# Attention: a running minimum of negated scores on VectorE in place of a pass over the blocks' maxima

## What is computed

```python
s = jnp.einsum('bqhd,bkhd->bhqk', qi, k, preferred_element_type=jnp.float32) * sc
s = s + (Fi[:, :, :, None] - Ft[:, :, None, :])
s = jnp.where(kpos[None, :] <= qpos[:, None], s, -jnp.inf)
pr = jax.nn.softmax(s, axis=-1)
return jnp.einsum('bhqk,bkhd->bqhd', pr.astype(v.dtype), v)
```

## Time and profile before

| | us |
|---|---|
| median of 3 runs | 1343.44 |
| lowest and highest | 1336.95, 1344.19 |
| profiled execution, whole time | 1337.98 |
| its span in the trace | 1336.3 |
| PE busy | 1273.1 (95%) |
| VectorE busy | 713.6 (53%) |
| ScalarE busy | 566.0 (42%) |
| GpSimd busy | 181.6 (14%) |
| mean granted clock of TensorE | 0.981 |

### The profile page before, as it was taken

One profiled execution on the slowest core, in us unless ns is written; L12 is line 12 of the kernel. 1 busy time (PEld: TensorE's weight loads), 2 busy tenths in 40 slices (PEclk: granted clock), 3 DMA queues, 4 the chain that ended last, 5 costly groups with the idle time before them and its releaser, 6 DMA issues. The chain is left out here.

```text
span 1336.3 us, 19347 instructions
## 1 busy us (share of the span) xinstructions
PE 1273.1 (95%) x7007; PEld 1033.3 (77%) x7007; DVE 713.6 (53%) x1965; ACT 566.0 (42%) x1158; POOL 181.6 (14%) x193
## 2 busy tenths in 40 slices
PE   6899999999999999999979999999999995899997
PEld 1669988888888888888857777777777774788885
DVE  0646531353465121100059889899898997244444
ACT  2536521221221212111148778787787886111111
POOL 1223310100100100110000041032013115000000
PEclk9899999999999999999969999999999999899999
DMA  9636454131122344331176859749677974666662
GB/s 364 240 114 198 146 159 139 51 97 64 34 97 66 123 148 130 125 123 64 50 200 80 124 111 152 112 100 171 85 123 126 103 186 117 205 197 195 199 192 63
DMA packets 163836, 179.51 MB, mean 134 GB/s; under 512 B 35361, under 2 KB 125013, under 8 KB 159974
## 3 DMA queue, kind: packets, MB, share of 16 engines
q1 hardware_dynamic: 158478, 160.42, 48.9%
q10 hardware_dynamic: 5264, 17.86, 4.2%
HBM read 111.55 MB, written 66.69 MB: 133 GB/s over the span
## 5 line engine op out<-in xcount | busy, mean ns | idle before, releaser
L597 PE MATMUL prj_acc<-prj_hhi,til_whi 128*128 128x512 f32 (+1 forms) x800 | 286.3, 358 | 0.0
L599 PE MATMUL prj_acc<-prj_hlo,til_whi 128*128 128x512 f32 (+1 forms) x800 | 284.3, 355 | 0.0
L598 PE MATMUL prj_acc<-prj_hhi,til_wlo 128*128 128x512 f32 (+1 forms) x800 | 284.2, 355 | 0.0
L1589 DVE TENSOR_TENSOR att_wlo<-att_tps,att_whi 128x512 fp32r<-128x512 f32 (+1 forms) x336 | 185.1, 584 | 25.4 <-ACT att_whi L1542 23.6
L1542 ACT ACTIVATE att_whi<-att_tps 128x512 fp32r<-128x512 f32 (+1 forms) x336 | 164.1, 516 | 43.7 <-PE att_ops L1494 21.8
L599 PEld LDWEIGHTS prj_acc<-prj_hlo,til_whi 128*128 128x128 f32 x800 | 150.8, 188 | 21.3
L597 PEld LDWEIGHTS prj_acc<-prj_hhi,til_whi 128*128 128x128 f32 x800 | 150.9, 189 | 20.9
L598 PEld LDWEIGHTS prj_acc<-prj_hhi,til_wlo 128*128 128x128 f32 x800 | 150.8, 188 | 20.7
L1579 DVE TENSOR_SCALAR_CACHE_REDUCE att_wx<-att_sps 128x512 f32<-128x512 f32 (+4 forms) x164 | 94.0, 595 | 103.7 <-PE att_sps L1466 98.8
L1463 PE MATMUL att_sps<-att_ka,att_qa 128*128 128x512 f32 (+4 forms) x328 | 135.4, 413 | 10.9 <-DMA att_kb<-scratch_fkd 10.5
L1494 PE MATMUL att_ops<-att_whi,att_vt 128*128 128x512 f32 (+1 forms) x336 | 138.1, 415 | 1.0 <-DVE att_wlo L1589 1.0
(11 more groups left out here) (189 smaller groups left out, 2073.0 us busy)
## 6 DMA issues: line engine op xcount, KB each, us to landing
til_wraw<-in_w_in SPq DMA_DIRECT2D x20, 512.0 KB, 4.2
scratch_v<-val_vs SPq DMA_DIRECT2D x17, 512.0 KB, 4.8
val_xt<-in_x_prompt ACTq DMA_DIRECT2D x16, 512.0 KB, 4.4
ini_al<-in_w_ada SPq DMA_DIRECT2D x8, 1024.0 KB, 16.3
zin_zh<-scratch_z SPq DMA_DIRECT2D x16, 512.0 KB, 4.4
zin_zl<-scratch_z SPq DMA_DIRECT2D x16, 512.0 KB, 5.7
zin_xr<-in_x_prompt SPq DMA_DIRECT2D x16, 512.0 KB, 5.5
out_y_prompt<-yo_o ACTq DMA_DIRECT2D x16, 512.0 KB, 2.8
```

The source lines that it names most:

```text
L597: pe.matmul(out, w[0][:, k, :], hhi[:, k, cs], start=(k == 0), stop=False)
L598: pe.matmul(out, w[1][:, k, :], hhi[:, k, cs], start=False, stop=False)
L599: mm = pe.matmul(out, w[0][:, k, :], hlo[:, k, cs], start=False, stop=(k == KT - 1))
L1589: dve.tensor_tensor(wlo[b][0:x.keys, x.skip:x.width], tps[x.i % T_RING][0:x.keys, x.skip:x.width], raw(whi[b][0:x.keys, x.skip:x.width]), ...
```

## The change

Scores are copied with the factor -1 in place of 1, and the instruction takes the minimum instead of the maximum. From a row's second block on it starts from the result of the block before it (`before`, a 128x1 operand in memory), and so it waits for that block (`s_free`). The last block of a row writes to `nm` directly. The TENSOR_REDUCE, its semaphore `row_ok` and the function `rows_done` are gone. ScalarE waits for the row's last block by `s_free`, and its exponential takes the negated scores with scale -1. In the planner, the 100 that a row's last block cost more than others is gone. All later lines move up by 5, so line 1589 is 1584 in the new file, 1542 is 1537 and 1536 is 1531.

```diff
         if kind == "den":
             return 300, 120
-        return (170 if kind == "score" and x.last else 70) + 103 * (x.width if kind == "add" else x.n) // 100, 120
+        return 70 + 103 * (x.width if kind == "add" else x.n) // 100, 120
...
                 if kind == "exp":
-                    act.wait_ge(row_ok, rows_done(st) - sum(b.last for b in st.blocks) + 1
-                                + [b.row for b in st.blocks if b.last].index(x.row))
+                    act.wait_ge(s_free, ROW_END[st.index, x.row] + 1)
...
-                    act.activation(w, w, ACT.Exp, bias=nm[0:x.m, e, x.row:x.row + 1],
+                    act.activation(w, w, ACT.Exp, scale=-1.0, bias=nm[0:x.m, e, x.row:x.row + 1],
...
+                    before = None
+                    if x.b >= 1:
+                        dve.wait_ge(s_free, x.i)
+                        before = top[0:x.m, e, x.row, x.b - 1:x.b]
+                    here = nm[0:x.m, e, x.row:x.row + 1] if x.last else top[0:x.m, e, x.row, x.b:x.b + 1]
                     dve.tensor_scalar(weights(st, x.row, x.w0, x.n), sps[x.i % S_RING][0:x.m, 0:x.n],
-                                      1.0, None, ALU.mult, ALU.max,
-                                      accum_out=top[0:x.m, e, x.row, x.b:x.b + 1]).then_inc(s_free, 1)
-                    if x.last:
-                        dve.wait_ge(s_free, x.i + 1)
-                        dve.tensor_reduce(nm[0:x.m, e, x.row:x.row + 1], top[0:x.m, e, x.row, 0:x.b + 1], AX, ALU.max,
-                                          negate=True).then_inc(row_ok, 1)
+                                      -1.0, before, ALU.mult, ALU.min, accum_out=here).then_inc(s_free, 1)
```

## The result

| | before | after |
|---|---|---|
| median, us (8 runs each) | 1343.24 | 1349.20 |
| lowest and highest, us | 1336.95, 1345.35 | 1346.15, 1351.75 |
| ratio after to before | | 1.0047, 95% interval 1.0027 to 1.0066 |
| profiled execution: span, us | 1336.3 | 1349.9 |

The changed kernel is 6 us slower; 1345 had been forecast. The profiled execution of before lies low in its spread and that of after high, so their spans differ by more than the medians. The clock is the same (0.98) and the merge takes as long as it did; the time is in the attention.

The account below looks back on a forecast made before the run. VectorE's queue and its holes were taken to bound the attention: 5.1 us less work, 8.1 us more holes, its end 3.0 us later within slack. The merge, 1.5 us later, gave 1345 us from a 1343.44 median; range 1333 to 1355.

Parts of the forecast that it names:

- Scalars: VectorE, 172 blocks behind another of their row: reading one scalar from memory adds 0.06 us each, 10.3 us.
- The wait: VectorE, 77 blocks directly behind their row's previous block: each starts 0.115 us later, 8.9 us in all.
- work term: VectorE's work in the attention: 24.3 us of reduces off, 10.3 and 8.9 us added; 5.1 us less.
- The six holes: Ends of steps 5, 8, 11, 14, 17, 20: VectorE idles 2.49 us instead of 1.14, net +8.1 us.
- PE's lost time: PE starves about a microsecond in each hole and may not make it up: 0 to 2.4 us, taken as 0.
- The handover: Attention to merge: a SyncE, GpSimd, DMA chain starts the merge, 2.6 - 1.1 = 1.5 us later.
- The hook: Where the merge's chain hangs on VectorE in head 5: 5 x 1.35 - 4.1 = 2.6 us later.
- Step 20's early reciprocals: They come right behind the step's last block, ending SyncE's 6.7 us wait; DMA lets 1.1 us be won.
- the first (waits free): New waits and scalars cost VectorE nothing, work falls 14 to 24 us; 1333 us, chance 0.12.
- the second: The hole on VectorE is smaller or regained while the 1.14 us stalls go; about 1336 us, chance 0.14.
- the fourth: The DMA chain has more slack against VectorE, so the merge starts as before; 1343 us, 0.52 together with the forecast.
- The third: PE's lost microsecond is not regained and some 14 step starts lose 0.5 us each; 1352 us, chance 0.22.

Follow-up runs that it names:

- the case of the pairs: The blocks of two rows alternate, so none directly follows the one whose minimum it takes, planner costs adjusted; against the kernel before: 1327.81 us, ratio 0.9905.

## Why the prediction was right or wrong

- **What bounds:** right that VectorE's queue sets most of the pace. Reduces taken off and waits put on moved the time by 0.5 to 0.8 of their size, scalars by 0.3.
- **Reduces removed:** 0.19 us each as work, right; the sum took them at full worth, the chip gave half (12.3 of 25.8 us over the whole kernel).
- **Scalars:** 0.06 us each, right (742 for 680 ns); at the end they cost 3.2 of 11.5 us.
- **The wait: a term that was mis-sized.** The working took 0.115 us from the reduce's start in the earlier trace rows; the direct pairs take 0.20 to 0.21. In 77 pairs that is 0.09 x 77 = 7 us more, and turns the work term of -5.1 us into about +2. In the old order, over the whole kernel, it is 20.5 + 11.5 - 25.8 = +6.2 us, and +6.3 was measured. That this fits so well is luck: in the medians the three terms showed as 16.1 + 3.2 - 12.3 = +7.0, each at another share of its size.
- **The six holes:** place and mechanism right, 2.12 us for 2.49 forecast, and the 1.14 us waits did go. VectorE stands ahead of the reciprocals, for the exponentials, and not ahead of the subtraction for whi. All waits for ScalarE rose to 42.8 us (some 38 forecast). Missed: the six waits of 0.99 us at the ends of first steps (the same cause, reciprocals right behind a last block) and the knock-on. The attention's end was to move by 3.0 us in all; the order alone moved it by 14.8, both by 24 to 26.
- **PE's lost time taken as 0:** wrong for the attention. "It may not make it up" was the right half of that sentence: PE's waits for VectorE's subtractions ahead of its transposes rose from 9.6 to 16.5 us, and VectorE in turn waited for PE's second score product 5.5 us (1.1 before). What it is worth by itself no run shows.
- **The handover: a step that failed.** It is right for the kernel before, and for the new instructions in the old order, that the merge is set by a chain with a hook on VectorE further back and not by the attention's end. For the changed kernel it is wrong. The end of the attention was to move by 3.0 us "inside the 13.5 us of slack"; it moved by 24 to 26, used the slack up, and holds the merge in both profiles: by the addition at 1137.53 in one, by the last subtraction and value products in the other. The merge was to start 1.5 us later and started 10 to 15 us later in these two profiles. The other chain was late too: by the estimate above it would have held the merge 1 to 2 us short of that.
- **The hook** was to come 2.6 us later and came 10.4 (392.1 for 381.7). The old order with the new instructions has 10.5, so the instructions suffice for it: the work term, which stood in the hook with -4.1. With 0.205 us for each of the old order's 89 pairs, the prediction's counts give 10.3 + 18.2 - 24.3 = +4.2 there; what makes 10.5 of it, beside the scatter of single profiles, stays open.
- **Step 20's early reciprocals:** right that the order moved them forward: with old instructions they come only 2.7 us later although the holes had opened. Wrong that SyncE's wait for them would go and the next reciprocals be sent sooner: SyncE waited 9.6 us for them (6.7 before), and the reciprocals of step 21, which it sends next, come 19.9 us later from the first block (408.2 for 388.3). For the order alone the steps of the text give 5 x 1.35 - 1.1 = 5.65 us; the hook moved by 2.7, the time by 1.9.
- **Rivals:** the first (waits free) is refuted by the kernels with and without the wait, 16.1 us apart; the second and the fourth by the sign. The third gave 1352 and is the nearest in time, but not by its mechanism: the waits for transposes at step starts went.
- The forecast of 1345 stood 4 us below the measured 1349, with the sign of the work term wrong and the merge of the changed kernel held by another chain. That it was so near is in part luck: the work term was too low, the order's part at the hook too high, and the attention's end, 24 to 26 us late, moved the merge only by what the 13.5 us of slack did not cover.

## What to carry to other kernels

Before a small pass is replaced by a chain through the main instructions, count how often a link stands directly behind the one before: here each such link cost 0.20 us of a full engine, and the pass that a row was rid of 0.19 us. If the order can put something between (two rows in turn, or a planner that knows of the wait), the same change turns from 6 us of loss into 8 to 13 of gain, of which the order by itself gave 4 in the case of the pairs. And follow every chain that the next stage hangs on, with its slack: before the change it was the one of reciprocals and gates, after it the end of the attention, and with other planner costs step 20's reciprocals, 0.2 us of work, came 7.7 us later and the merge 7.6, though the attention's end came earlier.

## What was not expected of the hardware

- A block copy from PSUM that waits for the accumulator read directly ahead of it starts 0.20 to 0.21 us after that read's start, with or without a scalar operand; without the wait both start together (0). A 128x4 TENSOR_REDUCE that waits for it starts 0.12 us after it (818.47 to 818.58 in the earlier trace rows is one of them).
- A scalar read from memory costs a 128x512 instruction from PSUM the same 60 ns as a 128x1 one: 62 ns by the medians. It is time of the engine: without waits such blocks follow each other at 0.67 us for 0.61.
